# A second, turned copy of the memory tokens loaded from HBM in place of sixteen transposes per layer

## What is computed

```python
h = h + concatenate([y_a, y_b, y_c]) @ w_mix_out[l]
h = h + memory_cross_attention(rms_norm(h, norm_ca[l]), rms_norm(mem, norm_mem[l]), w_ca_q[l], w_ca_kv[l], ...)

def memory_cross_attention(h_norm, mem_norm, w_q, w_kv, ...):
    q = (h_norm @ w_q).reshape(B, S, CA_HEADS, CA_HEAD_DIM)
    kv = (mem_norm @ w_kv).reshape(B, M, CA_HEADS, 2 * CA_HEAD_DIM)
    ...
```

## Time and profile before

| what | value |
|---|---|
| median of 3 runs | 1368.94 us (1368.78 to 1369.36) |
| the profiled execution's own time | 1369.13 us |
| its span, first to last instruction | 1367.4 us |
| PE busy | 1354.3 us (99%) |
| DVE, ACT, POOL busy | 959.4 us (70%), 700.9 us (51%), 512.6 us (37%) |
| chain that ended last | PE 95%, ACT 2%, DVE 2%, issue 1% |
| mean HBM rate over the span | 91 GB/s |

### The profile page before, as it was taken

The page is one execution under the profiler, slowest core; times in us unless marked ns, Lnnn a source line. Parts: engine busy times, 40 slices in busy tenths (PEclk is TensorE's granted clock), DMA queues, the critical chain, the costliest instruction groups (busy, mean ns, idle before and its releaser), DMA issues.

```text
span 1367.4 us, 19564 instructions
## 1 busy us (share of the span) xinstructions
PE 1354.3 (99%) x7631; PEld 1127.3 (82%) x7631; DVE 959.4 (70%) x1384; ACT 700.9 (51%) x1166; POOL 512.6 (37%) x323
## 2 busy tenths in 40 slices
PE   8999999999999999999999999999999999999999
PEld 6888788887889988988988877888778888888887
DVE  4583873765899479858985657836658895797587
ACT  6747583675444344334467465835754433434433
POOL 4645665642430232032036457656334203310420
PEclk9999999999999999999999999999999999999999
DMA  6332013332561565056033320133235705741731
GB/s 178 104 90 75 19 58 90 114 108 70 162 174 42 154 185 139 30 169 157 17 93 93 89 75 17 48 108 108 93 93 155 183 16 175 194 108 39 205 80 62
DMA packets 180924, 142.59 MB, mean 104 GB/s; under 512 B 15169, under 2 KB 153184, under 8 KB 180832
## 3 DMA queue, kind: packets, MB, share of 16 engines
q1 hardware_dynamic: 175664, 124.55, 30.5%
q0 software_dynamic: 4608, 16.78, 6.4%
q10 hardware_dynamic: 560, 0.01, 0.0%
HBM read 122.44 MB, written 2.10 MB: 91 GB/s over the span
## 4 chain that ended last, share of the span: by engine, by line
PE 95%; ACT 2%; DVE 2%; issue 1%; DMA 0%; POOL 0%; DVEq 0%; POOLq 0%
PE bank L777 28%; PE bank L779 28%; PE bank L778 28%; PE bank L929 1%; PE bank L1140 1%; PE bank L995 1%; PE bank L955 1%; PE bank L934 1%; PE bank L943 1%; PE bank L1300 1%; PE bank L1215 1%; PE bank L1062 1%; ACT Qx L1546 0%; PE bank L785 0%; PE bank L1106 0%
## 5 line engine op out<-in xcount | busy, mean ns | idle before, releaser
L701 POOL TENSOR_TENSOR w_lo<-raw,w_hi 128x1024 fp32r<-128x1024 f32 (+3 forms) x148 | 361.3, 2445 | 634.0 <-ACT w_hi L1416 632.1
L777 PE MATMUL bank<-x_hi,w_hi 128*128 128x512 f32 x944 | 371.5, 394 | 1.8 <-DVE x_lo L2157 1.4
L779 PE MATMUL bank<-x_hi,w_lo 128*128 128x512 f32 x944 | 367.5, 389 | 0.0
L778 PE MATMUL bank<-x_lo,w_hi 128*128 128x512 f32 x944 | 367.4, 389 | 0.0
L1416 ACT ACTIVATE w_hi<-raw 128x1024 fp32r<-128x1024 f32 (+2 forms) x181 | 189.6, 1047 | 124.2 <-PE bank L779 123.5
L777 PEld LDWEIGHTS bank<-x_hi,w_hi 128*128 128x128 f32 x944 | 177.2, 188 | 44.8 <-issue 5.4
L778 PEld LDWEIGHTS bank<-x_lo,w_hi 128*128 128x128 f32 x944 | 177.3, 188 | 37.4 <-issue 1.4
L779 PEld LDWEIGHTS bank<-x_hi,w_lo 128*128 128x128 f32 x944 | 177.2, 188 | 37.0
L779 PE MATMUL bank<-p_hi,w_lo 128*128 128x256 f32 x308 | 87.2, 283 | 0.0
L778 PE MATMUL bank<-p_lo,w_hi 128*128 128x256 f32 x308 | 87.2, 283 | 0.0
L777 PE MATMUL bank<-p_hi,w_hi 128*128 128x256 f32 x308 | 87.1, 283 | 0.0
(11 more groups left out here) (352 smaller groups left out, 2744.8 us busy)
## 6 DMA issues: line engine op xcount, KB each, us to landing
raw<-in_w_ffn_in SPq DMA_DIRECT2D x88, 512.0 KB, 4.1
w_lo<-raw POOLq DMA_DIRECT2D x32, 512.0 KB, 4.9
raw<-in_w_in SPq DMA_DIRECT2D x27, 512.0 KB, 3.8
raw<-in_w_mix_out SPq DMA_DIRECT2D x16, 512.0 KB, 3.9
raw<-in_w_ca_kv SPq DMA_DIRECT2D x32, 256.0 KB, 3.3
b_y<-in_w_ffn_out SPq DMA_DIRECT2D x10, 512.0 KB, 5.0
b_x<-in_w_ffn_out SPq DMA_DIRECT2D x10, 512.0 KB, 5.3
b_z<-in_w_ffn_out SPq DMA_DIRECT2D x10, 512.0 KB, 6.7
```

Of the source, the lines that this page charges most:

```text
L701: pool.tensor_tensor(w_lo[gi % SPLIT][:, c0:n], whole[:, c0:n], w_hi[gi % SPLIT][:, c0:n].bitcast(f32), ALU.subtract).then_inc(S["lo_split ...
L777: pe.matmul(o, ah, bh, start=first, stop=False, skip_group_check=shared_bank)
L778: pe.matmul(o, ah, bl, start=False, stop=False, skip_group_check=shared_bank)
L779: mm = pe.matmul(o, al, bh, start=False, stop=last, skip_group_check=shared_bank)
```

## The change

The host program lays the memory out a second time, turned (`mem_t`, 1024 x 256), as one more input. Each layer loads it into SBUF by one more DMA of 1 MB on SP's queue, right behind `mem_tok`, into space that is free there (`mem_t`, 8 KB per partition behind `mem_tok`). The sixteen transposes of a layer are gone, with their claims of the banks 4 to 7. ACT makes `m_hi` from `mem_t` in SBUF after one wait for the load, and DVE makes `m_lo` from `mem_t` in SBUF. `mem_tok` is still loaded, for the root mean squares.

```diff
-        mem_tok = place("mem_tok", R0, [P, MT, D])
+        mem_tok, mem_t = place("mem_tok", R0, [P, MT, D]), place("mem_t", R0 + 8, [P, KD, NM])
...
+                            sp.dma_start(mem_t[:, :, :], A["mem_t"].rearrange("(k p) m -> p k m", p=P)).then_inc(S["mem_t_in"], 16)
...
-                    def memory_turned():
-                        pe.wait_ge(S["mem_in"], past(layer, "mem_in") + 16 * MT)
-                        for c in range(KD // 2):
-                            claim(4 + c)
-                            for k in range(2):
-                                for m in range(MT):
-                                    mm = pe.transpose(pb[4 + c][:, k * NM + m * P:k * NM + (m + 1) * P],
-                                                      mem_tok[:, m, (2 * c + k) * P:(2 * c + k + 1) * P], ident[:, :])
-                            mark(mm, S["memT_mm"])
-                            freed[4 + c] = (S["m_lo_done"], past(layer, "m_lo_done") + 2 * c + 2)
-
-                    project("mix", KD, None, YA, 0, 1, before={3: memory_turned}, x2=YB, k2=NH)
+                    project("mix", KD, None, YA, 0, 1, x2=YB, k2=NH)
...
+                    act_.wait_ge(S["mem_t_in"], past(layer, "mem_t_in") + 16)
                     for k in range(KD):
-                        act_.wait_ge(S["memT_mm"], past(layer, "memT_mm") + k // 2 + 1)
-                        act_.activation(m_hi[:, k, :], pb[4 + k // 2][:, (k % 2) * NM:(k % 2 + 1) * NM], ACT.Copy,
+                        act_.activation(m_hi[:, k, :], mem_t[:, k, :], ACT.Copy,
                                         scale=gain_of(layer, "norm_mem", k)).then_inc(S["m_hi_done"], 1)
...
-                        dve.scalar_tensor_tensor(m_lo[:, k, :], pb[4 + k // 2][:, (k % 2) * NM:(k % 2 + 1) * NM], gain_of(layer, "norm_mem", k),
+                        dve.scalar_tensor_tensor(m_lo[:, k, :], mem_t[:, k, :], gain_of(layer, "norm_mem", k),
                                                  m_hi[:, k, :].bitcast(f32), ALU.mult, ALU.subtract).then_inc(S["m_lo_done"], 1)
...
+    laid["mem_t"] = np.swapaxes(np.asarray(inputs["mem"])[0], 0, 1)
```

More of the change, by code:

```diff
@@ L377, in build_trunk @@
             qk_prod pair_prod diag_mm diag_evac decays_done scores_base q_level k_level sweep_mm swept khat_t khat_evac u_mm state_done o_mm o_sq_done o_evac o_ss o_r o_done last_o_done yT_mm yT_hi yT_lo
-            proj_mm h_added mem_r memT_mm m_hi_done m_lo_done ckv_mm ckv_evac ck_ss ck_r ck_done ckT_mm ckT_evac
+            proj_mm h_added mem_r mem_t_in m_hi_done m_lo_done ckv_mm ckv_evac ck_ss ck_r ck_done ckT_mm ckT_evac
             cq_mm cq_evac cq_ss cq_r cqT_mm cqT_evac
@@ L474, in build_trunk @@
             gate_mm=1, diag_mm=2, score_mm=20, probsT_mm=20, pv_mm=MLA_PV + NH, sweep_mm=4 * len(LEVELS), khat_t=3, u_mm=NT - 1,
-            o_mm=NT, yT_mm=4, proj_mm=2 * H_ADDS, memT_mm=KD // 2, ckv_mm=2 * MT, cq_mm=NT, ckT_mm=2, cqT_mm=NT, ffn_mm=2 * FC,
+            o_mm=NT, yT_mm=4, proj_mm=2 * H_ADDS, mem_t_in=16, ckv_mm=2 * MT, cq_mm=NT, ckT_mm=2, cqT_mm=NT, ffn_mm=2 * FC,
             x_hi_done=3 * KD, cig_half=1, r_done=2, lat_sq_done=4, lat_hi_done=4, r_lat_done=1, rope_evac=1, q_evac=2 * NT, sq_done=2 * NT,
@@ L2458 @@
     arrays, aps = {}, {}
-    for name in _INS:
-        a = np.ascontiguousarray(inputs[name])
+    laid = {name: inputs[name] for name in _INS}
+    laid["mem_t"] = np.swapaxes(np.asarray(inputs["mem"])[0], 0, 1)
+    for name in laid:
+        a = np.ascontiguousarray(laid[name])
         arrays[f"in_{name}"] = a
```

## The result

The change makes the kernel slightly slower: 1372.05 us in the median of 15 runs (1370.0 to 1373.8), against 1369.35 us for the kernel before on the same chip (15 runs, 1368.61 to 1370.81). The ratio is 1.0019, with a 95% interval of 1.0013 to 1.0026. That is just within the 0.2% that the prediction called no change, but 0.85 us above the top of its range. Of the distance between the forecast 1369.8 and 1372.05, 0.41 us lies in the kernel before, whose median is 1369.35 in these 15 runs and was 1368.94 in the three that the prediction went by; the change itself costs 2.70 us, where +0.85 was forecast. The fastest of the 15 runs, 1370.0, comes near the predicted 1369.8; the typical run is some 2 us worse. The profiled execution is one of the better ones, 1370.7 us.

The account below looks back on a forecast made before the run. PE bounds the kernel, busy 99% of the span; removing transposes saves 3.5 us of its stream, but waiting for POOL makes the keys 0.44 and 0.41 us later: 1368.94 + 0.85 = 1369.8 us, range 1368.8 to 1371.2.

Parts of the forecast that it names:

- the wait takes the place of the transposes: Before the memory's keys, PE waits for the first m_lo, held by POOL's split: +0.4 to +1.7 us, chance 0.88.
- So whoever has two tensors in SBUF stands still until POOL is done: At the first m_lo on DVE: with both operands in SBUF it ends 0.28 us after POOL's weight split.
- the sums of squares: Second rival, at the third caq slab: DVE falls behind, sums come late, PE loses 2.7 us per layer; 1375.2, chance 0.05.
- The other edits: Reads from SBUF, the 1 MB mem_t load, later additions, dropped waits: nothing; 4.5 us if the weight slab's cover were gone.
- the third rival: PE's 2.1 us gap before the keys halves the clock for 48 matmuls: 10.9 us per layer, 1391 us, chance 0.02.

Follow-up runs that it names:

- the load alone: Kernel before, with mem_t also loaded behind mem_tok and ACT waiting for it, nothing reading it, transposes kept: 1370.42 us against 1369.79, ratio 1.0007.
- the load ahead: Changed kernel with the load of mem_t issued some 23 us earlier on SP, before its wait for the sweeps: 1373.11 us against 1369.79, ratio 1.0020.
- the repeated run: Changed kernel run again with no edit: median 1372.84 us against 1368.90 for the kernel before, ratio 1.0024; its profiled execution took 1372.77 us.

## Why the prediction was wrong

**Right: the wait takes the place of the transposes.** "So whoever has two tensors in SBUF stands still until POOL is done" holds, with the 0.28 us behind POOL's end read off the rows of `p_lo`. The first `m_lo` takes 1.92 us (forecast: about 2), PE stands 1.88 (2.1), the second keys matmul shifts by +0.46 and +0.30 (+0.44 and +0.41). Two later `m_lo` are drawn out as well, with no harm to the sums of squares. An undisturbed `m_lo` takes 0.47 us, not at most 0.41 as the prediction took over from `p_lo`, which changed nothing. The Trainium skill, "SBUF — State Buffer", section "Who interferes with whom", says that a DVE instruction with two inputs in SBUF contends with a POOL instruction that reads SBUF, over ports that are an exclusive lock. These runs agree: 1.92 us beside the split, and 0.48 with the split put behind it.

**Wrong: the step "The other edits", its sentence on the load of `mem_t`: "Nothing".** The cover that was named, ACT's use of the weight slab at 216.72, is real, and that slab did no harm. But it was the only client of the DMA engines that was asked about. Instructions, by our reading PE's own, travel on the same 16 engines, and in the second layer they had less slack than the weights: +0.8 us in the profiled execution, +0.63 in the medians of the load alone, whose interval just includes zero.

**Wrong: the third rival, "the clock falls in the gap", its chance of 0.02 and its price of 10.9 us per layer.** Two of the six gaps of 1.88 us in three profiles are followed by a fall, which costs 1.6 us. The mean clock was below 1.000 in 30 of the 37 runs with such gaps (19 of 26 of the changed kernel, 11 of 11 with the load ahead), against 33 of the 146 runs with gaps of about 1 us or less at the keys. Three readings led to the chance and the price. The price took all 48 matmuls of the keys at half clock, where the fall lasted for some eight of them. And "no slice with a lower clock" was taken for evidence against falls: a slice of the page is 1367.4 / 40 = 34 us long, and a fall to one half from 930.7 to 934.2 lowers its mean only to 0.95. The page of the repeated run, with two falls in it, also shows a 9 in every slice. And the wait of 1.35 us at 12.58, the other piece of evidence against a fall, came from one execution: at that very place the clock does fall in five of the twelve profiles. Priced at 1.6 us per fall, with the larger chance that the trace could not exclude, the rival would have carried the range to 1369.8 + 3.2 = 1373.0.

Added up: the wait +0.8, the stop +0.8 and one fall in a gap +1.6 make 3.2 us, and the fall at the program's start that the repeated run has in addition, +0.8, makes 4.0. That run is 1372.77 us, 3.9 above the median of before; the medians moved by 2.7 and 3.9 us.

What stays open: why a gap of 1.88 us lowers the clock in one layer and not in the other of the same execution, and whether the load ahead made falls behind the gap more frequent, or only the chip did. Falls in the gaps of both layers were not seen in one execution.

## What to carry to other kernels

Work that leaves the critical engine is a gain only if what it was hiding is ready: before removing it, look up who sets the next start, and move that producer first (here, making the halves 29 us earlier turned a loss of 2.7 to 3.9 us into a gain of 2.8). Count every client of a shared resource when a load is added, the instruction queues too; "issue" as a releaser together with a missing q8 row is how their lateness looks. And a gap on TensorE has two prices, its length and what the clock does behind it; the second is read in windows of a few microseconds and over several runs, never from the page's slices or one execution.

## What the runs showed of the hardware

- A gap of 1.88 us on PE, a thousandth of the program, was followed by a granted clock of 0.50 in two of six cases that were profiled, and 30 of 37 runs with such gaps lost some clock, against 33 of 146 without. Gaps of 0.1 to 1.2 us away from the program's start were not followed by a fall in any profile here; the two of 6.4 us both were. The Trainium skill, "TensorE: Matmul & The Clock Gate", section "What's actually happening", says that an idle TensorE falls back to the lower of its two clocks; here it is seen.
- DVE and POOL alternated one for one when both had work with SBUF operands at hand: with four splits queued, eight `m_lo` of 0.47 us took 11.83 us.
- A late block of instructions left PE idle for 0.3 to 1.2 us, and shows in no wait of the program.
